# A router that is read row tile by row tile, with two weight rests of the first expert on GpSimd

## The reference, cut to what matters

```python
hn = rmsnorm(h, norm_ffn_w)                        # 512 x 1024
g_prob = softmax(hn @ wrg + brg)                   # 4 groups
g_p, g_idx = top_k(g_prob, 1)
e_logits = (hn @ wre + bre).reshape(512, 4, 8)     # 32 experts
e_logits = take the 8 of group g_idx
e_p, e_idx = top_k(softmax(e_logits), 2)
weights = g_p * e_p / sum(e_p)
# each row goes to its two experts, and with x the rows of expert e:
y = (silu(x @ w_gate[e]) * (x @ w_up[e])) @ w_down[e]
out = h + sum of weights * y
```

## Time and profile before

| what | value |
|---|---|
| runs | 2268.79, 2273.22, 2272.18 us |
| median | 2272.18 us |
| profiled execution | 2272.49 us |
| its span | 2270.7 us |
| busy: PE, DVE, ACT, POOL | 2189.1, 1478.3, 1248.6, 303.6 us |
| router's first transpose to first gather | 1689.98 to 1723.57 us |
| first product of the experts | 1734.26 us |

### The profile page before, as it was taken

One profiled execution on the slowest core, in us unless ns is written; L12 is line 12 of the kernel. 1 busy time (PEld: TensorE's weight loads), 2 busy tenths in 40 slices (PEclk: granted clock), 3 DMA queues, 4 the chain that ended last, 5 costly groups with the idle time before them and its releaser, 6 DMA issues. The chain is left out here.

```text
span 2270.7 us, 31925 instructions
## 1 busy us (share of the span) xinstructions
PE 2189.1 (96%) x12430; PEld 1734.5 (76%) x12430; DVE 1478.3 (65%) x1868; ACT 1248.6 (55%) x1693; POOL 303.6 (13%) x346
## 2 busy tenths in 40 slices
PE   7999999999999999999999999999995999999998
PEld 6878658877768787998888888888684777777774
DVE  3533862548888778765324573443447999988897
ACT  4324552478884455652315423244434888888885
POOL 2000001023320122640000000000011111122220
PEclk9999999999999999999999999999996999999999
DMA  7122117423224434011222213333136999999996
GB/s 240 57 74 93 37 38 248 132 82 93 93 84 158 144 118 149 3 59 56 93 93 93 93 53 115 111 123 137 56 137 251 397 408 408 407 407 396 404 400 253
DMA packets 121731, 385.61 MB, mean 170 GB/s; under 512 B 9548, under 2 KB 38532, under 8 KB 96400
## 3 DMA queue, kind: packets, MB, share of 16 engines
q1 hardware_dynamic: 106688, 333.54, 39.9%
q0 software_dynamic: 14416, 44.12, 5.7%
q10 hardware_dynamic: 512, 6.34, 0.7%
HBM read 362.89 MB, written 28.89 MB: 173 GB/s over the span
## 5 line engine op out<-in xcount | busy, mean ns | idle before, releaser
L2404 DVE TENSOR_TENSOR w_lo<-raw,w_hi 128x2048 fp32r<-128x2048 f32 x117 | 268.7, 2296 | 454.6 <-ACT w_hi L1750 454.4
L1750 ACT ACTIVATE w_hi<-raw 128x2048 fp32r<-128x2048 f32 x117 | 223.9, 1913 | 405.1 <-PE bank L914 366.1
L914 PE MATMUL bank<-hT_hi,w_hi 128*128 128x512 f32 x512 | 201.2, 393 | 4.6 <-DVE hT_lo L2468 2.3
L914 PE MATMUL bank<-hT_hi,w_lo 128*128 128x512 f32 x512 | 200.3, 391 | 0.0
L914 PE MATMUL bank<-hT_lo,w_hi 128*128 128x512 f32 x512 | 200.3, 391 | 0.0
L1125 PE MATMUL bank<-hT_hi,w_hi 128*128 128x512 f32 x432 | 174.0, 403 | 0.9 <-DVE hT_lo L2468 0.9
L1125 PE MATMUL bank<-hT_hi,w_lo 128*128 128x512 f32 x432 | 168.4, 390 | 0.0
L1125 PE MATMUL bank<-hT_lo,w_hi 128*128 128x512 f32 x432 | 168.3, 390 | 0.0
L3267 DVE TENSOR_TENSOR e_lo<-eraw,e_hi 128x2048 fp32r<-128x2048 f32 x62 | 141.9, 2290 | 35.0 <-ACT e_hi L2293 35.0
L3151 DVE TENSOR_TENSOR e_lo<-raw,e_hi 128x2048 fp32r<-128x2048 f32 x64 | 146.5, 2289 | 8.6 <-ACT e_hi L2276 8.1
L3151 DVE TENSOR_TENSOR w_lo<-raw,w_hi 128x2048 fp32r<-128x2048 f32 x64 | 144.4, 2286 | 5.4 <-ACT w_hi L2276 5.3
(11 more groups left out here) (609 smaller groups left out, 5197.4 us busy)
## 6 DMA issues: line engine op xcount, KB each, us to landing
raw<-expert_w_gate SPq DMA_DIRECT2D x64, 1024.0 KB, 11.2
raw<-expert_w_up SPq DMA_DIRECT2D x64, 1024.0 KB, 11.6
eraw<-expert_w_down SPq DMA_DIRECT2D x62, 1024.0 KB, 11.2
raw<-w_in SPq DMA_DIRECT2D x40, 1024.0 KB, 5.1
raw<-even_w_in SPq DMA_DIRECT2D x18, 1024.0 KB, 5.2
raw<-odd_w_in SPq DMA_DIRECT2D x16, 1024.0 KB, 5.3
raw<-even_w_out SPq DMA_DIRECT2D x8, 1024.0 KB, 5.2
raw<-odd_w_out SPq DMA_DIRECT2D x8, 1024.0 KB, 5.0
```

Of the source, the lines that this page charges most:

```text
L914: mm = pe.matmul(out, st, mv, start=first and x == 0, stop=last and x == 2)
L1750: act.activation(split_to(m)[0][:], raw[n % RAW][:], ACT.Copy).then_inc(sem("hi_done"), 1)
L2404: dve.tensor_tensor(split_to(m)[1][:], raw[split_of[m] % RAW][:], f32(split_to(m)[0][:]), ALU.subtract).then_inc(sem("lo_done"), 1)
```

## The change

TensorE, ScalarE and VectorE take the router by row tiles: a tile is transposed into two banks, copied out as two halves of four features (ScalarE features 0 to 3, VectorE 4 to 7), and multiplied with the router's columns by itself. The transposes of tile 0 stand ahead of the last row tile of the attention's output product. On VectorE only the rest of piece 0 stands ahead of `logits`; the rests of pieces 1 and 2 are taken by GpSimd. Behind `tok_of`, `x_lo(0)` now stands between the two `d_lo` of expert 0.

```diff
 # GpSimd, behind the writes to hn_dram and the memset of xg
+        for u in (1, 2):
+            pool.wait_ge(sem("gu_hi"), u + 1)
+            pool.wait_ge(sem("gu_lo"), u)
+            pool.tensor_tensor(e_lo[u][:], eraw[u][:], f32(e_hi[u][:]), ALU.subtract).then_inc(sem("gu_lo"), 1)
         together(pool, 23)
 # TensorE
-        gemm(pn["xo"][1:2], attended, False)
-        stage(wait=False)
+        banks_free(pn["xo"][1])
+        gemm_unit(pn["xo"][1], 0, attended, False)
         first = 4 * (pn["xo"][0] % 2)
...
+        def turn_ffn(t):
             pe.wait_ge(sem("norm_rows"), at_row("ffn", t))
+            if t >= 2:
+                pe.wait_ge(*after("hnT_act", t - 1))
+                pe.wait_ge(*after("hnT_dve", t - 1))
+            for f in range(KD):
+                tr = pe.transpose(psum[first + 2 * (t % 2) + f // 4][:, (f % 4) * P:(f % 4) * P + P], xs[:, t, f * P:f * P + P], ident)
+            tr.then_inc(sem("hnT_pe"), 1)
+
+        def tile_logits(t):
+            pe.wait_ge(*after("hnT_act", t + 1))
+            pe.wait_ge(*after("hnT_dve", t + 1))
+            for k in range(KD):
+                mm = pe.matmul(psum[(first + 4) % 8][:, t * R:t * R + R], hnT[:, k, t * P:t * P + P], w_router[:, k],
+                               start=k + t == 0, stop=k + t == KD + NT - 2)
+            if t == NT - 1:
+                mm.then_inc(sem("rt_pe"), 1)
+
+        for t in range(NT):
+            if t == NT - 1:
+                last = panels[pn["xo"][0]]
+                pe.wait_ge(sem("evac_dve"), last["at"] + last["nj"])
+                turn_ffn(0)
+            gemm_unit(pn["xo"][1], 1, attended, False, js=(t,))
+        stage(wait=False)
+        turn_ffn(1)
         pe.wait_ge(*after("router_in", 16 * 5))
-        for k in range(KD):
-            pe.wait_ge(*after(("hnT_act", "hnT_dve")[k % 2], k // 2 + 1))
-            for t in range(NT):
-                mm = pe.matmul(psum[first][:, t * R:t * R + R], hnT[:, k, t * P:t * P + P], w_router[:, k], start=k + t == 0, stop=k + t == KD + NT - 2)
-        mm.then_inc(sem("rt_pe"), 1)
+        pe.wait_ge(sem("evac_dve"), panels[pn["xo"][1]]["evac_at"][0])
+        for t in range(NT):
+            tile_logits(t)
+            if t + 2 < NT:
+                turn_ffn(t + 2)
 # ScalarE
-        norm_rows("ffn", resid, added=pn["xo"][-1])
-        for f in range(0, KD, 2):
-            act.wait_ge(*after("hnT_pe", f + 1))
-            act.activation(hnT[:, f], psum[(4 * (pn["xo"][0] % 2) + f) % 8][:], ACT.Copy).then_inc(sem("hnT_act"), 1)
-        gu_hi(0, range(3), True)
+        def tile_T(t):
+            act.wait_ge(*after("hnT_pe", t + 1))
+            act.activation(hnT[:, 0:4, t * P:t * P + P], psum[4 * (pn["xo"][0] % 2) + 2 * (t % 2)][:].rearrange("p (f s) -> p f s", s=P),
+                           ACT.Copy).then_inc(sem("hnT_act"), 1)
+        norm_rows("ffn", resid, (0, 1), added=pn["xo"][-1])
+        act.wait_ge(sem("evac_dve"), panels[pn["xo"][-1]]["evac_at"][2])
+        square("ffn", resid, 2)
+        tile_T(0)
+        root("ffn", 2)
+        norm_rows("ffn", resid, (3,), added=pn["xo"][-1])
+        tile_T(1)
+        tile_T(2)
+        gu_hi(0, (0,), True)
+        tile_T(3)
+        gu_hi(0, (1, 2), True)
 # VectorE
-        norm_rows("ffn", resid, add=added(pn["xo"]), gain=ffn_gain)
-        for f in range(1, KD, 2):
-            dve.wait_ge(*after("hnT_pe", f + 1))
-            dve.tensor_copy(hnT[:, f], psum[(4 * (pn["xo"][0] % 2) + f) % 8][:]).then_inc(sem("hnT_dve"), 1)
+        def tile_T(t):
+            dve.wait_ge(*after("hnT_pe", t + 1))
+            dve.tensor_copy(hnT[:, 4:, t * P:t * P + P], psum[4 * (pn["xo"][0] % 2) + 2 * (t % 2) + 1][:].rearrange("p (f s) -> p f s", s=P)).then_inc(sem("hnT_dve"), 1)
+        add = added(pn["xo"])
+        for t in range(NT):
+            if t == NT - 1:
+                tile_T(0)
+            add(t)
+            if t:
+                scale("ffn", resid, t - 1, gain=ffn_gain)
+            variance("ffn", t)
+        tile_T(1)
+        scale("ffn", resid, NT - 1, gain=ffn_gain)
+        tile_T(2)
...
         own.wait()
-        gu_lo(0, range(3))
+        tile_T(3)
+        gu_lo(0, (0,))
         dve.wait_ge(*after("rt_pe", 1))
...
+        dve.wait_ge(sem("gu_lo"), 3)
         gu_lo(0, (3,))
-        d_lo(0, range(2))
+        d_lo(0, (0,))
         x_lo(0)
+        d_lo(0, (1,))
```

More of the change, by code:

```diff
@@ L197, in build @@
         "rt_act": ("ab_act", 2),
-        "summed": ("g_kv", 2 * HEADS),
+        "tok_there": ("g_kv", 2 * HEADS),
         "g_intra": ("rg_a", 2 * RB),
@@ L1601, in _ @@
-        turn_ffn(NT - 1, range(KD))
-        pe.wait_ge(*after("router_in", 16 * 5))
-        R = NG + NE
-        for k in range(KD):
-            pe.wait_ge(*after(("hnT_act", "hnT_dve")[k % 2], k // 2 + 1))
-            for t in range(NT):
-                mm = pe.matmul(psum[first][:, t * R:t * R + R], hnT[:, k, t * P:t * P + P], w_router[:, k], start=k + t == 0, stop=k + t == KD + NT - 2)
-        mm.then_inc(sem("rt_pe"), 1)
+        banks_free(pn["xo"][1])
+        gemm_unit(pn["xo"][1], 0, attended, False)
@@ new lines, in _ @@
+        first = 4 * (pn["xo"][0] % 2)
+        R = NG + NE
+        def turn_ffn(t):
+            pe.wait_ge(sem("norm_rows"), at_row("ffn", t))
+            if t >= 2:
[12 more added lines that the diff above has]
+                mm.then_inc(sem("rt_pe"), 1)
@@ L3166, in _ @@
         own.wait()
-        gu_lo(0, range(3))
+        tile_T(3)
+        gu_lo(0, (0,))
         dve.wait_ge(*after("rt_pe", 1))
         R = NG + NE
-        own.link(dve.tensor_tensor(logits[:], psum[4 * (pn["xo"][0] % 2)][:, 0:NT * R].rearrange("p (t n) -> p t n", n=R),
+        own.link(dve.tensor_tensor(logits[:], psum[(4 * (pn["xo"][0] % 2) + 4) % 8][:, 0:NT * R].rearrange("p (t n) -> p t n", n=R),
                                    b_router[:].unsqueeze(1).to_broadcast([P, NT, R]), ALU.add))
```

## The result

Over 22 runs of each on one chip the kernel after has a median of 2277.68 us (2273.11 to 2281.25), the kernel before 2273.32 us (2268.79 to 2278.23). The ratio is 1.0019, with a 95% interval of 1.0012 to 1.0026: 4.4 us more at the medians, 2.7 to 5.9 by the interval. The profiled execution of after took 2274.2 us, its span 2271.8.

A forecast was written before the change was run, and what follows sets the result against it. Experts bound by TensorE and, from about 1914 us, weight loads; ahead of them the `tok_of` chain counts. Router 5.3 us earlier, GpSimd's hold 8.6 later, order 0.4 later: 3.7 us on 2272.49, so 2276.2, range 2271 to 2280.5.

The forecast's parts named there:

- A shift of `tok_of` should reach the end nearly in full: Ahead of the experts: the gather waits for `tok_of`, and all engines and expert 2's loads follow behind it.
- Rival C: Expert loop's tail: the shift is absorbed by the loads that bound it, 2272.5 us; chance 0.09.
- Moving one alone would have won almost nothing: Ahead of `logits`: VectorE's rests and TensorE's router products end 0.4 us apart, so the change must move both.
- Router: Ahead of `logits`: with the router by tiles and two rests off VectorE, `logits` starts 5.3 us earlier, bounds 4.5 to 5.6.
- GpSimd's price: Rests of pieces 1 and 2: each 128x2048 subtraction on GpSimd takes 4.56 us, bounds 4.1 to 5.1.
- Rival B: GpSimd's two subtractions: slower than taken, 6.6 us each, so 4.2 us more for the two, 2280.4 us; chance 0.10.
- What it does to VectorE: Choice chain behind `logits`: VectorE's operations with two SBUF inputs wait for GpSimd's subtractions, 8.6 us later, net 3.3.
- Rival A: Choice chain: GpSimd doesn't hold VectorE, so only 5.3 us is won and 0.4 lost, 2267.6 us; chance 0.11.
- If VectorE slips in one operation more at the hand-over: Choice chain, between GpSimd's two subtractions: one more VectorE operation gets in, winning back 0.4 us.
- The rule weighed there: Choice chain: two-SBUF-input VectorE and SBUF-reading GpSimd instructions exclude each other for the whole instruction; shift 3.3 us.
- The order: Behind `tok_of`: the second `d_lo` behind `x_lo(0)` makes ScalarE wait for `pair_T`; 0.4 us later, bounds 0.8 later, 0.6 earlier.
- no longer meets the gather, worth up to 1 us of its 7.86: Behind `tok_of`: the load of expert 1's last piece avoids the gather, up to 1 us won against `pair_T`'s 0.8 us.

The follow-up runs named there:

- tiles_only: The kernel after with GpSimd's two subtractions back on VectorE ahead of `logits`, router by tiles kept; ratio to the kernel before 1.0002 (0.9991 to 1.0014).
- gpsimd_only: The kernel before with only the rests of pieces 1 and 2 moved to GpSimd, router and order as before; ratio to before 1.0017 (1.0006 to 1.0028).
- quarters: The kernel after with each GpSimd subtraction cut into four parts of 128x512, no wait between them; ratio to the kernel before 1.0014 (1.0005 to 1.0024).
- old_order: The kernel after with both `d_lo` of expert 0 ahead of `x_lo(0)` again; ratio to the kernel before 1.0013 (1.0003 to 1.0023).
- gpsimd_copies: The kernel after with GpSimd copying raw pieces 1 and 2 in place of subtracting; ratio to the kernel before 0.9991 (0.9981 to 1.0001).

## Why the prediction was right, point by point

The forecast was 3.7 us more than the profiled execution, 2276.2; the medians differ by 4.4, and after's is 2277.68. The mechanism held; sizes were off, in both directions, and that the trace's sum of 3.77 us came within 0.1 of the forecast is partly luck: the router gave 0.94 less than forecast, the hold took 1.38 less, and the way behind `tok_of` took 0.51 more, for another reason than forecast.

*The bound.* "A shift of `tok_of` should reach the end nearly in full": it does, by the last table. Rival C (absorbed by the loads of the tail) falls with it. "Moving one alone would have won almost nothing" is what `tiles_only` and `gpsimd_only` show.

*Router, the term that was mis-sized: 5.3 us forecast, 4.36 measured,* just below its own lower bound of 4.5. The working said that the last tile's eight products, at 0.11 each, end by 1699.0 and lie hidden behind the rest of piece 0. The earlier trace rows has 64 products for four tiles, and that makes 16 for a tile, not 8: the trace shows each of these product calls as two (the transposes as one). A tile's products so take 1.87 us and not 0.9. This was off twice. TensorE reaches tile 3's transposes later, so that VectorE's copy of tile 3 ends 13.24 us behind the anchor (forecast 12.87), and `logits` waits another 0.54 for TensorE, which the forecast had ready 0.8 ahead. 0.37 + 0.54 = 0.91 of the missing 0.94 us. Steps ahead of it held: the last addition +0.93 (forecast 0.95), the last scaled rows +1.17 (1.25).

*GpSimd's price* was forecast as 4.56 us, measured 4.50 and 4.49. Rival B (6.6 each) falls. The Trainium skill's GPSIMD Engine Reference, "Elementwise — side-by-side cycle accounting", has 4497 ns, and the trace agrees.

*What it does to VectorE: 8.6 us forecast, 7.22 measured.* Rival A, that GpSimd doesn't hold VectorE, needed the chain to keep its 17.3 us; it has 24.56, and 17.11 as soon as GpSimd doesn't read. That a hold lasts 4.5 us and not only 1.4 was the open point; 3.60, 4.19 and 4.08 us settle it. Of the 1.4 us by which the hold was oversized, 0.4 is the slip that the text named ("If VectorE slips in one operation more at the hand-over"): L3225 got in between the two subtractions, the reduction L3226 needs no second input, and so L3227 and not L3225 was the one to be held the second time. Some 0.5 more is the late `logits`: GpSimd began 0.39 us ahead of it in place of 0.1 behind, so a part of its time was over before anything could be held. Another 0.27 is an idle moment in the chain of before that after's doesn't have. The rest, 0.2, is GpSimd's own: its two subtractions took 0.13 us less than twice 4.56, and the second held operation ended 0.03 us behind GpSimd's and not 0.2, less 0.07 for a longer step from one subtraction to the next. Late logits and a shorter hold are the same half microsecond seen twice, which is why the net of both, 2.86 us, is near to the 3.3 forecast.

The rule weighed there, that of the Trainium skill's SBUF — State Buffer, "Who interferes with whom", agrees with every run here: the hold lasts to the end of the instruction (of 4.5 us; of 1.23 in quarters), a GpSimd operation that only writes doesn't hold (0.17 us under both fills), and VectorE's reductions and bank readers go on (`logits` at 0.31, L3223 at 0.17).

*The order: 0.4 us forecast, 0.91 measured* from `tok_of` to expert 1's first product, 0.1 above its bound of 0.8. The step by which `pair_T` moves past ScalarE's split, 0.8 us on the path, was right and is found as a floor 0.74 to 0.9 higher. What failed is the other half of the term, that the load "no longer meets the gather, worth up to 1 us of its 7.86": in the nine traces in which the gather is in the chain it took 7.75 to 8.05 us with before's order and 7.47 to 8.33 with after's, so no gain shows. And in the profiled execution of after itself the floor isn't what set the time: 14 slow products did. So the 0.91 us of this pair are the clock's and not the order's, and that they lie near the forecast is luck. What decides between 7 and 14 of them I haven't found. In after TensorE stood idle for 14.17 us in the chain and its clock was at the lower of its two levels when the experts began; in some traces it rose 3 us after that, in others 6.

## What to carry over

Work that is moved to an idle engine is only free if the two engines don't meet at the memory (SBUF): GpSimd may fill or wait beside a chain of VectorE operations with two SBUF inputs, but a subtraction of 4.5 us by GpSimd held such a chain for 3.4 to 4.0 us, and cutting it in quarters won back 1.1 us of 7.2. Before moving work to another engine, look for idle time of the same engine a few steps later: here VectorE had 6 us behind `tok_of`, and the rests put there turned a loss of 4 us into a gain of some 3 (by the ratio; 1.6 by the medians, 4.3 in the trace). And count instructions by the trace's number, not the code's: a loop of 32 calls that shows as x64 costs 64.

## What the runs showed of the hardware

A GpSimd copy with one input holds VectorE like a subtraction with two, 1.57 us of its 1.89. The rows on which the forecast rested had not shown it for a copy. A held operation is shown as busy, from when it is issued to its end, so VectorE's share in 1697 to 1706 us reads 8.79 of 9.00 for seven operations. Between two GpSimd operations with a semaphore wait between them, 0.15 us apart, one further VectorE operation with two inputs gets in behind the held one (L3225, 0.17 us, in `after`, `old_order` and `gpsimd_copies`). TensorE began the experts at about 0.63 us for a 128x512 product in every trace, and came to 0.39 after 7 to 14 of them; each slow one costs 0.19 us where TensorE is the bound. The granted clock can fall with TensorE busy without a gap: it did 4.9 us (before) and 4.0 us (`gpsimd_only`) after the first of 64 router products of 36 columns, which from then on took 0.21 us in place of 0.11.
